# GpSimd centers two quarters of each inner norm and makes the feed-forward stages' sums over convolution states

## The reference

```python
def _layer_norm(x, g, b):
    xf = x.astype(jnp.float32)
    mu = jnp.mean(xf, axis=-1, keepdims=True)
    var = jnp.mean(jnp.square(xf - mu), axis=-1, keepdims=True)
    return ((xf - mu) * lax.rsqrt(var + LN_EPS) * g + b)

def _conv_ffn(x, conv0, w_up, conv_w, conv_b, w_down):
    h = x @ w_up
    h, conv_new = _causal_dwconv(h, conv0, conv_w, conv_b)
    g, u = jnp.split(h, 2, axis=-1)
    return (jax.nn.silu(g) * u) @ w_down, conv_new

x = _layer_norm(DN_ALPHA * x + sublayer(x), g[layer], b[layer])
```

## Time and profile before

| | |
|---|---|
| runs before | 3031.64, 3033.02, 3035.35 us |
| profiled execution | 3028.36 us, span 3026.7 us |
| TensorE busy | 2995.5 us (99%) |
| VectorE busy | 1971.8 us (65%) |
| ScalarE busy | 1622.9 us (54%) |
| GpSimd busy | 177.6 us (6%) |
| clock granted to TensorE | full throughout |

### The profile page before, as it was taken

How to read it: one execution, slowest core, us unless ns; L and a number is a source line. 1 busy time by engine, 2 the same in 40 slices (tenths; PEclk the granted TensorE clock), 3 DMA queues, 4 the chain that set the end, 5 groups by cost and what they waited for, 6 DMA issues and landing times.

```text
span 3026.7 us, 60182 instructions
## 1 busy us (share of the span) xinstructions
PE 2995.5 (99%) x25090; PEld 2927.2 (97%) x25090; DVE 1971.8 (65%) x2512; ACT 1622.9 (54%) x1741; POOL 177.6 (6%) x315
## 2 busy tenths in 40 slices
PE   9999999999999999999999999999999999999999
PEld 9999899999999999999999999999999999999998
DVE  5455454677665565767767888877686566657566
ACT  4435576545444444545556767775454444445454
POOL 1010101000000000000002222210000000000000
PEclk9999999999999999999999999999999999999999
DMA  7465667544444445554467887875444444446552
GB/s 280 181 237 205 225 223 283 197 156 166 178 168 181 200 171 202 186 182 166 155 226 260 271 307 270 293 261 196 180 163 181 183 191 166 180 189 200 180 193 100
DMA packets 101333, 615.41 MB, mean 203 GB/s; under 512 B 12992, under 2 KB 13264, under 8 KB 40112
## 3 DMA queue, kind: packets, MB, share of 16 engines
q1 hardware_dynamic: 69840, 500.33, 44.6%
q0 software_dynamic: 31328, 112.71, 11.3%
HBM read 575.70 MB, written 37.28 MB: 203 GB/s over the span
## 4 chain that ended last, share of the span: by engine, by line
PE 89%; DVE 6%; DMA 2%; ACT 2%; issue 1%; DVEq 0%; POOL 0%; ACTq 0%; POOLq 0%; SPq 0%
PE acc L675 28%; PE acc L677 27%; PE acc L676 27%; DVE lo L580 1%; DMA extra<-xds 1%; PE aux L2195 1%; DVE x L1889 1%; ACT hi L570 1%; DVE xl L1894 1%; PE aux L2544 0%; PE aux L2525 0%; DMA raw<-in_w 0%; ACT xh L1262 0%; DVE x L1883 0%; PE aux L2280 0%
## 5 line engine op out<-in xcount | busy, mean ns | idle before, releaser
L675 PE MATMUL acc<-xh,hi 128*128 128x264 f32 x7552 | 2178.2, 288 | 11.5 <-DVE lo L580 4.0
L677 PE MATMUL acc<-xh,lo 128*128 128x264 f32 x7552 | 2145.0, 284 | 0.0
L676 PE MATMUL acc<-xl,hi 128*128 128x264 f32 x7552 | 2141.5, 284 | 0.0
L675 PEld LDWEIGHTS acc<-xh,hi 128*128 128x128 f32 x7552 | 1423.6, 189 | 33.7 <-issue 21.0
L676 PEld LDWEIGHTS acc<-xl,hi 128*128 128x128 f32 x7552 | 1420.3, 188 | 1.8
L677 PEld LDWEIGHTS acc<-xh,lo 128*128 128x128 f32 x7552 | 1420.5, 188 | 0.0
L580 DVE TENSOR_TENSOR lo<-raw,hi 128x2048 fp32r<-128x2048 f32 x473 | 1077.2, 2286 | 373.3 <-ACT hi L570 372.5
L570 ACT ACTIVATE hi<-raw 128x2048 fp32r<-128x2048 f32 x473 | 896.9, 1905 | 483.3 <-DMA raw<-in_w 319.0
L569 ACT ACTIVATE xh<-pj 128x1056 fp32r<-128x1056 f32 x144 | 156.0, 1083 | 333.8 <-PE acc L677 275.5
L577 DVE TENSOR_TENSOR xl<-pj,xh 128x1056 fp32r<-128x1056 f32 x144 | 180.6, 1254 | 199.9 <-ACT hi L570 197.4
L1578 DVE SCALAR_TENSOR_TENSOR stage<-acc,par,stage 128x255 f32<-128x255 f32 x352 | 168.6, 479 | 23.4 <-DVE stage L1578 21.9
(11 more groups left out here) (302 smaller groups left out, 1639.3 us busy)
## 6 DMA issues: line engine op xcount, KB each, us to landing
raw<-in_w SPq DMA_DIRECT2D x473, 1024.0 KB, 4.9
x<-in_ssm POOLq DMA_DIRECT2D x32, 512.0 KB, 7.5
out_ssms<-x POOLq DMA_DIRECT2D x32, 512.0 KB, 7.7
x<-in_ret POOLq DMA_DIRECT2D x16, 512.0 KB, 5.4
out_rets<-x POOLq DMA_DIRECT2D x16, 512.0 KB, 4.3
x<-in_ck POOLq DMA_DIRECT2D x16, 512.0 KB, 4.9
x<-in_cv POOLq DMA_DIRECT2D x16, 512.0 KB, 5.8
pj<-cumd POOLq DMA_DIRECT2D x32, 256.0 KB, 7.4
```

The lines of the kernel that those rows point to most:

```text
L675: pe.matmul(out, hi[:, s, w], xh_k, start=kc == 0 and k == 0, stop=False)
L676: pe.matmul(out, hi[:, s, w], xl_k, start=False, stop=False)
L677: m = pe.matmul(out, lo[:, r, w], xh_k, start=False, stop=kc == ph.kc - 1 and k == CK - 1)
```

## The change

In norms 0, 1 and 2 quarters three and four are centered by GpSimd (`centered`), with one instruction of 128x1056 each, as soon as `lsum` is there; VectorE waits for them (`ln_moved`) before it scales the quarter. In both feed-forward stages the three instructions of 128x704 over convolution states move from VectorE to GpSimd, behind the centerings. `lvar` is kept on another row of pj, since the sums now are written while it is still in use. The counts of `ln_fin` and `ln_moved` follow from that.

```diff
-        lvar = [pt[:, LP + (6 if l == 1 else 3), :] for l in range(4)]
+        lvar = [pt[:, LP + (3 if l == 3 else 6), :] for l in range(4)]
...
+            def centered(l):
+
+                pool.wait_ge(R["ln_delta"], l + 1)
+                for q in (2, 3):
+                    v = x[:, CK * q:CK * q + CK, :]
+                    pool.tensor_tensor(v, v, lsum[:, :].unsqueeze(1).to_broadcast([P, CK, T]), ALU.add)\
+                        .then_inc(R["ln_moved"], 1)
+
             def ffn(layer):
...
                 pool.dma_start(fst, d["fst"][layer]).then_inc(R["ffn_state_in"], 16)
+                centered(2 * layer)
+                pool.wait_ge(R["ffn_state_in"], 16 * (layer + 1))
+                for k, o in ((0, fsum), (1, ftmp)):
+                    w = fcw[:, layer, k, :].unsqueeze(2).to_broadcast([P, 2 * FT, NB])
+                    pool.tensor_tensor(o, fst[:, :, k, :], w, ALU.mult).then_inc(R["ffn_sum"], 1)
+                pool.wait_ge(R["ffn_sum"], 3 * layer + 2)
+                pool.tensor_tensor(fsum, fsum, ftmp, ALU.add).then_inc(R["ffn_sum"], 1)
...
             pool.dma_start(sst, d["sst"]).then_inc(R["sconv_in"], 16)
+            centered(1)
             pool.wait_ge(R["ln_a"], 2 * KT)
...
-                dve.wait_ge(R["ln_moved"], 1)
+                dve.wait_ge(R["ln_moved"], 7)
...
                     if q == XB - 1:
                         split_lo(dve, lead[l][3][0], Step(0), 3, None)
-                    center(q)
-                    dve.wait_ge(R["ln_fin"], fin + CK + 1 + q)
+                    if q == 1:
+                        center(q)
+                    else:
+                        dve.wait_ge(R["ln_moved"], 2 * l + q - 1)
                     scale_tile(CK * q)
...
                 dve.wait_ge(R["ffn_state_in"], 16 * (layer + 1))
-                for k, o in ((0, fsum), (1, ftmp)):
-                    w = fcw[:, layer, k, :].unsqueeze(2).to_broadcast([P, 2 * FT, NB])
-                    tt(o, fst[:, :, k, :], w, ALU.mult).then_inc(R["ffn_sum"], 1)
-                dve.wait_ge(R["ffn_sum"], 3 * layer + 2)
-                tt(fsum, fsum, ftmp, ALU.add).then_inc(R["ffn_sum"], 1)
                 dve.wait_ge(R["ffn_sum"], 3 * layer + 3)
```

More of the change, by code:

```diff
@@ L1849, in final_norm @@
                 dve.reciprocal(rinv, lvar[l]).then_inc(R["ln_fin"], 1)
-                dve.wait_ge(R["ln_fin"], 8 * l + 2)
+                dve.wait_ge(R["ln_fin"], 6 * l + 2)
                 def wide(k):
@@ L1883, in center @@
                     tt(v, v, every(lsum[:, :]), ALU.add).then_inc(R["ln_fin"], 1)
+                    dve.wait_ge(R["ln_fin"], fin + CK + 2)
                 def center_tile(t):
@@ L1895, in low_tile @@
                     ins.then_inc(R["x_lo" if t % CK == CK - 1 else "x_first"], 1)
-                fin = 8 * l
+                fin = 6 * l
                 center_tile(0)
```

## The result

The changed kernel has a median of 3039.63 us over 18 runs (3035.85 to 3046.98), the kernel before, on the same chip, 3032.19 us over 18 (3028.15 to 3038.29). The ratio is 1.0024 with a 95% interval of 1.0017 to 1.0031, or **7.3 us slower** (5.2 to 9.4). The forecast was 8.6 us.

The account below looks back on a forecast made before the run. TensorE was taken as the bound, with VectorE pacing the seams; 3.9 us at up0, 3.9 at up1 and 0.8 at bc made +8.6 us on a median of 3033.02, so 3041.6 us, range 3024 to 3046.5.

Parts of the forecast that it names:

- The bound, and where it counts: TensorE busy 2995.5 of 3026.7 us; VectorE changes count only where TensorE waits, at three inner seams.
- the two engines take turns: At the seams, two-SBUF-input VectorE instructions and GpSimd's exclude each other for whole instructions; +8.6 us, chance 0.55.
- VectorE is never held: Rival at the seams: only the gain of 8.4 us is left, 3024.6 us; chance 0.20.
- VectorE goes first: Rival at the seams: GpSimd gets the gaps, about +3 at up0 and up1, 3038.4 us; chance 0.13.
- GpSimd's work is dearer: Rival at up0 and up1: 2.32 us a sum instruction, +4.8 us on the forecast, 3046.4 us; chance 0.12.
- The sizes at up0: Delays at the seam to up0 from taking turns, less the relief: net +3.9 us, the same at up1.
- first product: At up0, the low half that starts TensorE, and so its first product, comes 5.6 us late.
- evacuation of bank 0: At up0, ScalarE frees bank 0 3.9 us late, and TensorE's restart follows it.
- the 704-column instruction: Each GpSimd sum over convolution states at up0 and up1 takes 1.51 us, holding VectorE as long.
- The relief: Work gone from VectorE at the seams: quarters three and four gain 0.6 and 1.3 us, ScalarE's sum wait goes.
- Bc: Seam to bc, centerings only: 2.7 us late, less 0.6 and 1.3, so +0.8 us.
- Code loading: At up0's seam, GpSimd's first instruction might load code and start later: up to 1.5 us more.

Follow-up runs that it names:

- e3: The changed kernel, but VectorE's centerings and scalings read one of their two operands from PSUM; ratio 0.9997 to the kernel before.
- e8: The changed kernel with e3's PSUM inputs, GpSimd's centerings and sums placed beside other VectorE work, quarters three and four centered by GpSimd; ratio 0.9984 to before.
- e4: The changed kernel with more TensorE filler products during the norm wait, 10 at norms 0 and 2, 6 at norm 1; ratio 1.0018 to before.
- e1: The changed kernel with the sums over convolution states back on VectorE, only the centerings on GpSimd; ratio 1.0010 to the kernel before.
- e6: The changed kernel, but GpSimd starts only when quarter one's low halves are done; ratio 1.0039 to the kernel before.

## Why the prediction was right, and where its terms were off

**The bound, and where it counts**, held. TensorE is 99% busy in both kernels, and what the change gained and cost on VectorE shows in TensorE's time at the three seams.

**That the two engines take turns** held instruction by instruction, in both directions. The row of norm 3 had shown GpSimd waiting; the converse, which the prediction took from the likeness of the instructions, is shown by e3. Of its first two rivals, "VectorE is never held" is excluded by the 2.64 us row, and "VectorE goes first" by the scaling that lasts 1.51 us with GpSimd's first sum beside it. The third, that GpSimd's work is dearer (3.48 and 2.32 us), is excluded by e8, where the instructions take 2.43 and 1.41. Its price was also too low: it counted the longer sums alone, and the same reading makes each of the six centerings 1.2 us longer too.

**The sizes at up0**, each against the row of before, relative to `lsum`:

| step | predicted, us | measured, us |
|---|---|---|
| scaling of tile 0 ends late by | 0.5 | 0.35 |
| first product | 5.6 | 4.73 |
| VectorE at quarter two | 7.1 | 6.22 |
| TensorE at quarter two | 7.1 | 7.46 |
| ScalarE's high half | 5.2 | 4.19 |
| evacuation of bank 0 | 3.9 | 2.78 |
| TensorE's restart | 3.9 | 4.11 |

The term that was mis-sized is **the 704-column instruction**. I scaled 2.27 us by its columns to 1.51. What it held VectorE for was 1.02, 1.13 and 1.47 us, 3.6 in place of 4.5. The centering was right (2.21 us of delay against 2.27). The whole chain through VectorE and ScalarE came out about a microsecond earlier than I had said. The relief was sized well: VectorE's lateness falls by 0.75 us to quarter three and by 1.28 to quarter four (0.6 and 1.3 predicted), and TensorE gets back 3.35 us between quarter two and the restart (3.2 predicted).

The step that was missing is **the clock**. I worked out that TensorE would stand for over 5 us and went on at its full pace of 5.9 us a quarter. Its rows show half the granted clock for the next 6 us, and e4 puts that at 1.15 us here. The two errors nearly cancel: 3.9 predicted, 4.11 measured. That this figure came out so close is luck. With the clock kept up (e4) TensorE starts quarter two 6.24 us late, as late as VectorE's low halves, waits for nothing behind it and so gets back 3.28 us: the restart is +2.96 us, a microsecond less than my step, and nearly all of that microsecond is the sums'. I had also named the evacuation of bank 0 as what the restart follows; it is only 2.78 us late, and TensorE comes to it later than that.

**Bc**: first product 2.7 predicted, 2.57 measured; restart 0.8 predicted, 1.39 measured. e4 takes 0.85 us off and leaves 0.55, so the step itself was close and the clock was again what was missing. **Up1**: 3.9 predicted, 3.58 measured, 2.95 in e4. In sum 8.6 predicted, 9.1 in the seams of the profiled execution, 7.3 (5.2 to 9.4) in the medians.

**The relief** came as said: at up0 and up1 no wait of ScalarE for the sums, and at no seam one of TensorE at the restart. **Code loading** at the first GpSimd instruction doesn't show: the configuration instruction stood at 683.7 for 37 ns, and the centering began at 685.25, 0.09 us behind the end of `lsum`'s row. The Trainium skill, "GPSIMD Engine Reference", section "Instruction dispatch", has some 6 us before the first call of freshly loaded code; this trace shows none of it, so it disagrees, or the code wasn't freshly loaded, and no run here tells which.

What stays open is the size of the part outside the seams. The medians and the seams agree within the interval, and I made no run on the stages between bc and norm 2.

## What to carry to other kernels

Work moved to GpSimd isn't off VectorE's path if both read two tensors in SBUF: count nearly the whole GpSimd instruction against the VectorE instruction that it meets (here 2.21 us for one that takes 2.43 by itself, and 1.02 to 1.47 for one of 1.41), and look for what lies beside it at that very moment, not for GpSimd's idle share. Place it under VectorE instructions with one SBUF input (a reciprocal, an operand left in PSUM), and the same work becomes a gain: 7.3 us lost in the change as made, some 5 us won with the same GpSimd instructions in other places and one VectorE operand in PSUM. When an estimate says that TensorE will stand for some microseconds, add what the lower clock then costs behind it (0.6 to 1.15 us a seam here).

## What was unexpected of the hardware

- **The clock fell after short stands.** Filler products ran at the full clock until some 5 us (up0) and 2.8 us (e1) before the next product; in the 6 us behind it, and in e1 in the 3 us, the granted clock was 0.50 and 0.53 in the mean. In e3 it stayed at 1.00 after a stand of 1.46 us and fell to 0.50 after one of 1.83. The price in the kernel after was 0.6 to 1.15 us a seam, less than the products themselves lost (28 starts 0.10 us further apart than at full clock at up0, some 2.8 us), since VectorE was late as well.
- **The turns are even.** With both engines having work in hand, neither kept its place for two instructions: in the rows of after, one VectorE instruction goes between each two of GpSimd.
- **GpSimd loses too.** Its two centerings took 5.24 us in after, 5.93 in e6 and 4.80 in e3; one of e8, with no VectorE instruction of two SBUF inputs beside it, takes 2.43.
